# A two-layer transformer block on one core: last chunks by token halves, and a one-column stationary in the opening

## The reference, cut to what matters

```python
mod = silu(c) @ w_mod + b_mod                    # c is one row of 2048; w_mod 2048 x 12288
shift_a, scale_a, gate_a, shift_m, scale_m, gate_m = split(mod, 6)
h = rmsnorm(x, pre_mix_g) * (1 + scale_a) + shift_a
proj = h @ w_in
...                                              # latent attention, gated linear attention
x = x + gate_a * rmsnorm(mix @ w_out, post_mix_g)
h = rmsnorm(x, pre_mlp_g) * (1 + scale_m) + shift_m
x = x + gate_m * rmsnorm(relu(h @ w_up)**2 @ w_down, post_mlp_g)
# second block: rmsnorm, projections w_in_2, windowed attention and convolution, then
x = x + rmsnorm(merged @ w_out_2, mix_post_g_2)
x = x + rmsnorm((silu(gate) * up) @ w_down_2, ffn_post_g_2)   # gate, up = rmsnorm(x) @ w_gate_up_2
```

## Time and profile before

| | |
|---|---|
| median of three runs | 2870.9 us (2863.7 to 2878.3) |
| profiled execution | 2896.2 us, span 2894.4 us |
| TensorE busy, matmul and load | 95%, 81% |
| DVE, ScalarE, GpSimd busy | 64%, 42%, 1% |
| granted TensorE clock, mean | 0.965 of 2.4 GHz |
| HBM read | 560 MB, 194 GB/s over the span |

### The profile page before, as it was taken

How to read it: one execution, slowest core, us unless ns; L and a number is a source line. 1 busy time by engine, 2 the same in 40 slices (tenths; PEclk the granted TensorE clock), 3 DMA queues, 4 the chain that set the end, 5 groups by cost and what they waited for, 6 DMA issues and landing times.

```text
span 2894.4 us, 38739 instructions
## 1 busy us (share of the span) xinstructions
PE 2750.6 (95%) x14509; PEld 2357.5 (81%) x14509; DVE 1860.6 (64%) x2341; ACT 1214.6 (42%) x1553; POOL 21.9 (1%) x41
## 2 busy tenths in 40 slices
PE   7998899996999999999979999998979999999998
PEld 7886679885888888888768878887868888888886
DVE  4568788787986445654446878867455555655444
ACT  3144353144443444444344434454454444444443
POOL 1000000000000000000010000000000000000000
PEclk9789999997999999999989999999989999999999
DMA  7777786366786666665655645555545656655664
GB/s 260 269 273 260 231 251 208 102 214 237 241 282 196 196 191 187 186 189 192 195 138 169 193 140 169 169 155 170 175 129 183 187 183 188 186 183 182 192 194 152
DMA packets 434372, 564.19 MB, mean 195 GB/s; under 512 B 17959, under 2 KB 305123, under 8 KB 433744
## 3 DMA queue, kind: packets, MB, share of 16 engines
q1 hardware_dynamic: 432768, 559.76, 61.1%
q0 software_dynamic: 1488, 2.84, 0.4%
HBM read 560.43 MB, written 2.10 MB: 194 GB/s over the span
## 4 chain that ended last, share of the span: by engine, by line
PE 85%; DVE 6%; ACT 3%; DMA 3%; issue 2%; SPq 0%; ACTq 0%; DVEq 0%
PE ps L671 33%; PE ps L673 17%; PE ps L689 9%; PE ps L691 9%; PE ps L690 9%; PE ps L853 2%; DVE mod_acc L1521 2%; PE ps L994 2%; DMA mod_w<-in_w_mod 2%; DVE w_lo L1462 1%; ACT w_hi L1112 1%; DMA w_raw<-in_w_in 1%; ACT ring L1217 1%; DMA w_raw<-in_w_out 1%; PE ps L724 1%
## 5 line engine op out<-in xcount | busy, mean ns | idle before, releaser
L1462 DVE TENSOR_TENSOR w_lo<-w_raw,w_hi 128x1024 fp32r<-128x1024 f32 (+1 forms) x872 | 1052.6, 1212 | 763.5 <-ACT w_hi L1109 401.2
L671 PE MATMUL ps<-acts,w_hi 128*128 128x512 f32 x4224 | 1515.7, 403 | 16.3 <-DVE w_lo L1462 9.0
L673 PE MATMUL ps<-acts,w_lo 128*128 128x256 f32 x4224 | 1191.1, 282 | 0.0
L671 PEld LDWEIGHTS ps<-acts,w_hi 128*128 128x128 f32 x4224 | 801.7, 190 | 217.3 <-issue 17.4
L1112 ACT CAST w_hi<-w_raw 128x1024 fp32r<-128x1024 f32 (+2 forms) x560 | 580.8, 1042 | 725.5 <-PE ps L673 644.4
L673 PEld LDWEIGHTS ps<-acts,w_lo 128*128 128x128 f32 x4224 | 805.9, 191 | 2.2 <-issue 1.7
L1109 ACT CAST w_hi<-w_raw 128x1024 fp32r<-128x1024 f32 (+1 forms) x312 | 323.1, 1039 | 531.2 <-PE ps L691 399.1
L689 PE MATMUL ps<-w_hi,ff 128*128 128x512 f32 x864 | 336.3, 389 | 0.0
L691 PE MATMUL ps<-w_hi,ff 128*128 128x512 f32 x864 | 336.1, 389 | 0.0
L690 PE MATMUL ps<-w_lo,ff 128*128 128x512 f32 x864 | 336.1, 389 | 0.0
L690 PEld LDWEIGHTS ps<-w_lo,ff 128*128 128x128 f32 x864 | 162.2, 188 | 33.8
(11 more groups left out here) (278 smaller groups left out, 1773.7 us busy)
## 6 DMA issues: line engine op xcount, KB each, us to landing
w_raw<-in_w_in SPq DMA_DIRECT2D x232, 512.0 KB, 3.9
w_raw<-in_w_down SPq DMA_DIRECT2D x216, 512.0 KB, 4.3
mod_w<-in_w_mod SPq DMA_DIRECT2D x192, 512.0 KB, 5.4
w_raw<-in_w_gate_up SPq DMA_DIRECT2D x176, 512.0 KB, 3.6
w_raw<-in_w_up SPq DMA_DIRECT2D x128, 512.0 KB, 4.1
w_raw<-in_w_out SPq DMA_DIRECT2D x64, 512.0 KB, 4.6
w_raw<-in_w_attn_o SPq DMA_DIRECT2D x16, 512.0 KB, 3.6
w_raw<-in_w_conv_o SPq DMA_DIRECT2D x16, 512.0 KB, 4.1
```

The lines of the kernel that those rows point to most:

```text
L671: pe.matmul(ps[:, bank, :], hi, lin_.act[:, kk, :, :], start=at_first, stop=False, skip_group_check=True)
L673: mm = pe.matmul(ps[:, bank, 0:T], lo, lin_.act[:, kk, 0, :], start=False, stop=at_last, skip_group_check=True)
L1462: dve.tensor_tensor(low[cut], raw[cut], high[cut].bitcast(F32), ALU.subtract).then_inc(lo_ready, 1)
```

## The change

1. **Opening.** A scale piece is no longer eight matmuls with 128 columns of w_mod stationary and one column of silu(c) moving, but two with that column of silu(c) stationary and 512 columns of w_mod moving, summed into one row of PSUM bank 6. After a block's eight pieces ScalarE copies the row to `scale_row`, and `block_columns` (in place of `shift_sums`) turns it into four columns with one-row matmuls after the shift sums; both go to bank 7. Of the chunks of the block before, number 4 is now run ahead of the sums and not behind them.
2. **Token halves.** In the last panel of the four projections the last four chunks run for tokens 0 to 127 and then again for 128 to 255. Squares, roots, weighing, residual and scaling go by halves. The next phase's first four chunks are no longer rounded ahead but within the boundary: chunk 0 between the halves, chunks 1 to 3 between groups of four tiles. The transposes put two tiles in a bank and all of the first eight run without waiting for low parts. The stores go out by halves.

```diff
+        scale_row = mod_acc[0:1, 1, 0:NW]
...
+                self.first_half = count("first_half", 1)
+                self.half_added = count("y_half_added", 1 if partial else 0)
                 self.squared = count("y_squared", 8)
-                self.weighed = count("y_weighed", 4)
-                self.stat = count("y_stat", 3)
+                self.weighed = count("y_weighed", 5 if partial else 4)
+                self.stat = count("y_stat", 6)
...
+        last_of = {"w_or": o_1, "down_1": o_2, "out_2": o_3, "down_2": o_4}
...
+                half, quarter = divmod(g, 4)
...
-            def token_chunk(ph, j):
+            def token_chunk(ph, j, halves=(0, 1)):
...
-                pe.wait_ge(lo_ready, chunk_seq(ph, 0, j) + 1)
+                if halves[0] == 0:
+                    pe.wait_ge(lo_ready, chunk_seq(ph, 0, j) + 1)
...
-                    for half in range(2):
+                    for half in halves:
...
-                mm.then_inc(chunk_used, 1)
+                if halves[-1] == 1:
+                    mm.then_inc(chunk_used, 1)
+                elif j == ids[-1]:
+                    mm.then_inc(last_of[ph.name].first_half.sem, 1)
...
-                for j in chunk_ids(ph, b):
+                ids = chunk_ids(ph, b)
+                by_half = ids[-SLOTS:] if ph.name in last_of and b == ph.n_panels - 1 else []
+                for j in ids[:len(ids) - len(by_half)]:
                     if b == 0 and ph.name in ready:
                         pe.wait_ge(*ready[ph.name](sum(ph.chunks[j][1:])))
                     token_chunk(ph, j)
                     beside(ph, j, True)
+                for half in range(2):
+                    for j in by_half:
+                        token_chunk(ph, j, (half,))
...
-                    if k >= 4:
-                        pe.wait_ge(*(t.ring if t.shift else t.lo)(k - 3))
-                    pe.wait_ge(*t.scaled(2 * (k // 4) + 2))
+                    if k >= 8 and k % 2 == 0:
+                        pe.wait_ge(*(t.ring if t.shift else t.lo)(k - 6))
+                    pe.wait_ge(*t.scaled((3, 4, 6, 8)[k // 4]))
                     for half in range(2):
-                        mm = pe.transpose(ps[:, 4 + k % 4, half * P:(half + 1) * P],
-                                          t.xh[:, half, k * P:(k + 1) * P], ident)
+                        c = k % 2 * T + half * P
+                        mm = pe.transpose(ps[:, 4 + k // 2 % 4, c:c + P], t.xh[:, half, k * P:(k + 1) * P], ident)
                     mm.then_inc(t.turned.sem, 1)
...
-                if p == 0 and block >= 2:
-                    pe.wait_ge(mods_done, block - 1)
+                if p == 0 and block:
+                    pe.wait_ge(row_out, block)
                 for k in range(2):
-                    for i in range(4):
-                        mm = pe.matmul(ps[:, 6 + block % 2, i:i + 1],
-                                       mod_w[:, slot, k * NW + i * P:k * NW + (i + 1) * P],
-                                       silu_c[:, DT + 2 * p + k:DT + 2 * p + k + 1],
-                                       start=p == 0 and k == 0 and i == 0, stop=p == BLOCK_PIECES - 1 and k == 1,
-                                       skip_group_check=True)
+                    mm = pe.matmul(ps[0:1, 6, :], silu_c[:, DT + 2 * p + k:DT + 2 * p + k + 1],
+                                   mod_w[:, slot, k * NW:(k + 1) * NW], start=p == 0 and k == 0,
+                                   stop=p == BLOCK_PIECES - 1 and k == 1, skip_group_check=True)
                 mm.then_inc(scale_used, 1)
...
-            def shift_sums(block):
+            def block_columns(block):
                 pe.wait_ge(shift_used, 2 * BLOCK_PIECES * (block + 1))
+                if block:
+                    pe.wait_ge(mods_done, block)
                 for i in range(4):
-                    mm = pe.matmul(ps[:, 6 + block % 2, 4 + i:5 + i], mod_acc[:, 0, block % 2 * NW + i * P:block % 2 * NW + (i + 1) * P],
-                                   ones[:, 0:1], start=False, stop=True, skip_group_check=True)
+                    pe.matmul(ps[:, 7, 4 + i:5 + i],
+                              mod_acc[:, 0, block % 2 * NW + i * P:block % 2 * NW + (i + 1) * P],
+                              ones[:, 0:1], start=i == 0, stop=True, skip_group_check=True)
+                pe.wait_ge(row_out, block + 1)
+                for i in range(4):
+                    mm = pe.matmul(ps[:, 7, i:i + 1], scale_row[:, i * P:(i + 1) * P], ones[0:1, 0:1],
+                                   start=False, stop=True, skip_group_check=True)
                 mm.then_inc(mod_mm, 1)
...
-                shift_sums(0)
+                block_columns(0)
...
-                        opening_chunk(block - 2, 4)
                         opening_chunk(block - 2, 5)
...
-                    shift_sums(block)
-                opening_chunk(BLOCKS - 2, 4)
+                    opening_chunk(block - 1, 4)
+                    block_columns(block)
                 opening_chunk(BLOCKS - 2, 5)
...
+            def square_last(o, ph, half):
+                b = ph.n_panels - 1
+                act.wait_ge(*o.squared(2 * b + half))
+                if o.partial:
+                    if half:
+                        act.wait_ge(summed, panel_seq(ph, 0, b) + 1)
+                    else:
+                        act.wait_ge(*o.half_added(1))
+                    src = o.y[:, half, b * NW:(b + 1) * NW]
+                else:
+                    if half:
+                        act.wait_ge(chunk_used, chunk_seq(ph, 0, ph.n_chunks - 1) + 1)
+                    else:
+                        act.wait_ge(*o.first_half(1))
+                    src = ps[:, 2 * bank_pair(ph, b) + half, :]
+                act.activation(square, src, ACT.Square,
+                               accum_out=y_sums[:, half, b:b + 1]).then_inc(o.squared.sem, 1)
+            def square_stream(o, t, half):
+                for quarter in range(4):
+                    n = 4 * half + quarter
+                    act.wait_ge(*o.added(n + 1))
+                    if quarter:
+                        act.wait_ge(*t.squared(n))
+                    act.activation(square, x_tok[:, half, quarter * NW:(quarter + 1) * NW], ACT.Square,
+                                   accum_out=x_sums[:, half, quarter:quarter + 1]).then_inc(t.squared.sem, 1)
+            def scale_half(t, half, quarter):
+                act.wait_ge(*t.stat(3 * half + 3))
+                cut = slice(quarter * NW, (quarter + 1) * NW)
+                act.activation(t.xh[:, half, cut], x_tok[:, half, cut], ACT.Identity,
+                               scale=x_root[:, half:half + 1]).then_inc(t.scaled.sem, 1)
...
+                    act.wait_ge(scale_used, BLOCK_PIECES * block)
+                    if block > 1:
+                        act.wait_ge(mod_mm, block - 1)
+                    act.copy(scale_row, ps[0:1, 6, :]).then_inc(row_out, 1)
...
+            def boundary(o, t, before, ph):
+                square_last(o, before, 0)
+                root(y_root[:, 0:1], o.stat, 0)
+                square_stream(o, t, 0)
+                act.wait_ge(*t.squared(4))
+                square_last(o, before, 1)
+                root(x_root[:, 0:1], t.stat, 0)
+                root(y_root[:, 1:2], o.stat, 1)
+                scale_half(t, 0, 0)
+                round_chunk(ph, 0, 0, True)
+                square_stream(o, t, 1)
+                root(x_root[:, 1:2], t.stat, 1)
+                scale_half(t, 1, 0)
+                scale_half(t, 0, 1)
+                scale_half(t, 1, 1)
+                for quarter in range(4):
+                    if quarter:
+                        round_chunk(ph, 0, quarter, True)
+                    turn_high(t, range(4 * quarter, 4 * quarter + 4))
+                    if quarter < 2:
+                        scale_half(t, 0, quarter + 2)
+                        scale_half(t, 1, quarter + 2)
+            def finish(o, ph):
+                for half in range(2):
+                    square_last(o, ph, half)
+                    root(y_root[:, half:half + 1], o.stat, half)
...
+            def half_root(sums, ap, stat, half):
+                link(dve.tensor_reduce(ap[:, half:half + 1], sums[:, half, :], AX.X, ALU.add))
+                dve.tensor_scalar(ap[:, half:half + 1], ap[:, half:half + 1], 1.0 / D, EPS, ALU.mult,
+                                  ALU.add).then_inc(stat.sem, 1)
+            def half_inverse(ap, stat, half):
+                dve.wait_ge(*stat(3 * half + 2))
+                dve.reciprocal(ap[:, half:half + 1], ap[:, half:half + 1]).then_inc(stat.sem, 1)
+                dve.wait_ge(*stat(3 * half + 3))
+            def add_last(o, ph, half):
+                b = ph.n_panels - 1
+                if o.partial:
+                    if half:
+                        dve.wait_ge(chunk_used, chunk_seq(ph, 0, ph.n_chunks - 1) + 1)
+                    else:
```

(70 more changed lines are left out.)

120 lines of the change are left out of this document (44 added, 76 removed).

## The result

| | before | after |
|---|---|---|
| median, runs of the two side by side | 2877.5 us (2863.7 to 2880.1, 5 runs) | 2856.8 us (2848.8 to 2857.7, 5 runs) |
| ratio, with 95% interval | | 0.9932 (0.9907 to 0.9957): 12 to 27 us faster |
| the same, measured again with the experiments | 2879.1 us (30 runs) | 2854.8 us (7 runs), 0.9934 (0.9909 to 0.9958) |
| profiled execution, span | 2894.4 us | 2847.0 us |

The change gains about 20 us (19 to 20 by the two ratios, 21 and 24 by the two pairs of medians). 38 were forecast, 2833 us. The two profiled executions differ by 47.4 us: the first profile of before (2896.2 us) was 18.8 us above the mean of all the 70 runs of that kernel that there are by now (2877.4 us), and above each of them.

What follows compares the result with a forecast made beforehand. TensorE was taken as the bound, 85% of the span, with its clock lowered in the opening. 27 us there and 10.7 at the boundaries made 38 off a median of 2870.9: 2833 us, range 2818 to 2860.

Steps and rivals of the forecast that it cites:

- block 0: First block of the opening: 11.9 us gained at full clock, nothing at half clock; 8 us taken.
- the block by hand: Opening, engine timeline worked out: block 1 takes 31.3 us, blocks 2 and 3 take 33.9 us each.
- The clock: Opening: the new scale pieces keep TensorE at 2.4 GHz in blocks 1 to 3, 1.72 us a piece.
- the thin stationary: Opening: the reason given for the clock holding, a stationary of few columns and all 128 rows.
- Rival (a): Opening: load round trips through two slots set the blocks, 2.8 us gained in each of three; 2852 us, chance 0.18.
- The tail: After the opening's last block: 0.5 us gained, as chunk 0 waits for its mods with only chunk 5 as cover.
- The boundaries: Ends of the four projections: half 0's norm runs under pass two; 1.0 + 3.4 + 3.4 + 2.9 = 10.7 us gained.
- the 1.7 to be given back at the bias loads: Second boundary: TensorE's wait grows from 2.3 to 4.0 us, cutting the gain of 5.1 to 3.4.
- (b): Opening: one stationary column does not hold the clock, every piece takes 3.4 us; 18 us slower, 2889 us, chance 0.07.
- (c): Boundaries: the smaller stock of loaded chunks gives gains back, 4 us left in all; 2840 us, chance 0.13.
- the signs to look for: After-profile: clock near 1.00, 34 us blocks, no load lull over 2 us, transposes at 9 to 10 us, 8 us end.
- The chances for faster: Whole kernel: 0.85 for faster, from the forecast (0.62), (c) and two thirds of Rival (a).

Runs made afterwards that it cites:

- halves alone: The kernel before with only the token halves edits, its opening left as it was: 2863.8 us, ratio 0.9944 to the kernel before.
- opening alone: The kernel before with only the opening's edits, its boundaries left as they were: 2865.3 us, ratio 0.9966 to the kernel before.
- new order: The changed kernel with chunk roundings and remainders reordered at the three inner boundaries, chunk 0 under the second pass: 2844.6 us, 0.9881 of before.
- eight slots: The changed kernel with eight slots for the opening's pieces in place of four: 2833.2 us, ratio 0.984 to the kernel before.
- the run with a wide one: The changed kernel with silu(c)'s column repeated 128 times as stationary, still 512 columns moving: 2854.9 us, 0.991 of before.

## Why the prediction was wrong, point by point

The opening by stretches, in us. "Old" is the mean of four profiles with the old opening (before three times, halves alone), "new" of four with the new one (opening alone, after twice, new order). Their ranges for block 0 are 44.6 to 51.6 and 38.4 to 40.2.

| | old | new | gained | forecast |
|---|---|---|---|---|
| block 0 | 48.1 | 39.4 | 8.6 | 8 |
| block 1 | 35.5 | 35.2 | 0.4 | 4.3 |
| block 2 | 39.3 | 36.7 | 2.6 | 7.3 |
| block 3 | 39.8 | 35.5 | 4.3 | 7.1 |
| behind it | 38.0 | 40.5 | -2.5 | 0.5 |
| sum | 200.7 | 187.3 | 13.4 | 27 |

**The step that failed** is the block by hand, 31.3 and 33.9 us: it laid out the loads through two slots too early, and TensorE's own work at its shortest. The three blocks come out at 35.2, 36.7 and 35.5 us, 8.3 us more in all. The working let the pieces' loads land 5.3 to 5.6 us behind the issue. The load behind piece 2, which stands on the chain in each of blocks 1 to 3, takes 6.54, 6.86 and 6.61 us in the first profile of after. In block 2 it is issued at 88.95 behind loads that are still under way, the last of which lands at 94.50, and it lands at 95.81; the loads ahead of it come in 1.3 to 1.4 us apart as well. The two loads on the chain make 1.2 of the 1.9 us by which block 2 is too long, and the rest is TensorE's own: on the chain its pieces take 1.82 to 1.88 us for 1.72, and a chunk takes 2.9 for 2.7.

The working had 3.8 us of waiting for loads (0.8, 1.9 and 1.1) in a block of 33.9, and in blocks 2 and 3 TensorE's idle time is not above that (3.5 and 2.8 by the mean of the four). What grew there is its busy time, 33.2 and 32.8 us for 30.1: longer pieces and chunks, and after half of the waits of 2 us and more a slip to 1.2 GHz, which the working did not have. In block 1 three of the four profiles begin with 1.8 to 2.4 us of waiting for DVE's last shift part, and in the first profile of after the load of that part (4.72 us) stands on the chain ahead of it. With eight slots the blocks are 0.5, 2.2 and 2.2 us below the working, so it is the two slots that cost it.

The clock, the step that the prediction doubted most, was right in size: blocks 1 to 3 together were granted 0.94 to 0.98. Its reason, the thin stationary, was not (the run with a wide one). Rival (a), with a chance of 0.18, named the round trip, and its price for the three blocks, 8.4 us, stands beside 7.3 measured. That the two agree is in part luck: it had 2.8 for each block, and 0.4, 2.6 and 4.3 were gained. It was dismissed because the lulls in the earlier trace rows show SyncE waiting for TensorE. They do, and in the changed kernel too. Both hold in turn: early in a block the loads run dry while TensorE works up to piece 0, and later they queue at 400 GB/s while TensorE waits. Rival (a) in turn was wrong to give block 0 nothing.

Block 0 gained 8.6 for 8, and that is luck in part: the prediction had it end at 43.6 in place of 51.6. It ends at 39.4, near the 39.7 worked out for full clock, in place of 48.1.

**The second part of the error is the sample.** Blocks 2 and 3 were taken at 41.2 and 41.0 us from one profile; the mean of four is 39.3 and 39.8, 3.1 us less to gain. That profile was 25 us above the median shown, and the prediction took its microseconds off the median without asking where the 25 lay. 13 of the 21 us by which it exceeds the two later ones lay in the opening. The median of three was itself 6.5 us below the mean of 70 runs, so 2833 would have been 2839 from that base.

**The tail** of the opening, 0.5 gained by the forecast, lost 2.5. TensorE waits 2.10 us up to 154.93 for the first remainder of the last block: with chunk 4 ahead of the sums only chunk 5 covers the way over DVE and ScalarE. The wait was named and priced at nearly nothing. The row of after, and then the tail with all engines in after, with chunk 4 behind the sums, and with eight slots:

```profile
154.93 0.47 PE L696 MATMUL ps<-w_hi,acts 128*128 128x512 f32 x1 [2.10 <-DVE w_lo L1535]
...
146.16:186.68 40.52, 36.72 (x174) 30.74 (x174) 22.61 (x36) 23.52 (x35) 0.00 (x0) 0.96 0.62 223
...
149.92:190.56 40.64, 38.06 (x173) 32.55 (x173) 23.12 (x37) 23.62 (x35) 0.00 (x0) 0.92 0.65 221
...
131.57:170.51 38.94, 35.13 (x173) 29.56 (x173) 22.28 (x35) 23.52 (x35) 0.00 (x0) 1.00 0.58 204
```

The wait alone does not make the loss. With chunk 4 behind the sums it is gone, and the tail is still 40.6 us, at a granted clock of 0.92. In this profile with eight slots the wait is there but the clock is not lowered, and the tail is 38.9. So the wait and the clock behind it cost the 2.5 us together, and putting chunk 4 back does not win them.

Together 8.3 + 3.1 + 3.0 - 0.6 (block 0 gave a little more) = 13.8, which is the 13.6 us missing in the opening up to rounding.

**The boundaries** were right in mechanism and close in size, 10.7 forecast. By chunk 2 behind the last matmul: first 37.5 to 33.9, less 2.4 to 3.6 us by which w_or ends later (44.4 to 44.7 us from the spreading of the row to the last matmul with the old kernel, 47.1 to 48.0 with the changed one; but also 47.2 with the opening alone and 47.5 with the halves alone, so it is not shown whose it is), so 0 to 1 for 1.0. Second 31.7 to 26.1, 5.6 for 5.1, and the 1.7 to be given back at the bias loads was not given back, the wait staying at 2.0 and 2.3 in the two profiles. Third 29.2 to 26.2, 3.0 for 3.4. End 10.85 to 7.3, 3.5 for 2.9. In all 12 to 13, and 16 (9 to 23) by the runs of the halves alone. Measured up to the first bias product the second boundary gives more: 210.2 to 214.7 us in the four profiles with the old boundaries, 203.7 to 206.1 in the eight with the halves in their first order, 7.5 by the means.

**Rivals.** (b) fell: 1.86 us a piece, 2.66 would have been needed. (c) fell for the change as it stands and shows only in the shorter boundary of the new order. Of the signs to look for, the clock, the 9 us to the transposes, the 3 us of waiting for DVE and the 8 us at the end came; the blocks of 34 us and the wait of 4 us at the bias loads did not. The load line came out between: the lull of block 2 is down to under 2 us, but in block 3 nothing is moved from 117.0 to 119.25.

**Its sums.** The lower end of the range, 2818, needs the upper bound of 35 us for the opening and 17 for the boundaries; block 0 wholly at full clock gives 31 and 2823. The chances for faster add up to 0.87 and not 0.85. Neither touches the forecast.

What is left between 26 (opening and boundaries by the means of profiles, 13.4 + 12 to 13) and 19 to 24 by the runs is inside the intervals; it was not traced further.

## What to carry to other kernels

A bound that is lifted uncovers the next one: before crediting a stage with what its engine is spared, lay out the loads as the new, faster engine would ask for them, with everything in flight at the same time, and see which piece waits for which slot. Price a change against several executions; where the profiled one is far above the median, find the stretch that holds the excess first, since it may be the one that is to be changed. And when the gain stays small, try the next bound with one edit: four more slots turned some 10 us into 24.

## What the runs showed of the hardware

**Two rates at one clock.** In the loop of gate_up TensorE is busy without a break, granted 1.00 throughout, and does the same work; yet it has two rates, and an execution keeps one of them to the end of the loop. All engines between 2160 and 2600 us: busy and count of TensorE matmuls, loads, DVE, ScalarE, GpSimd, then clock, DMA share, GB/s. First after, then before (a second profile):

```profile
2160.00:2600.00 440.00, 440.00 (x2536) 388.23 (x2535) 265.45 (x277) 197.56 (x221) 0.00 (x0) 1.00 0.63 189
```

```profile
2160.00:2600.00 440.00, 440.00 (x2492) 381.56 (x2491) 260.84 (x273) 192.56 (x215) 0.00 (x0) 1.00 0.59 186
```

2536 matmuls against 2492 in the same 440 us, 1.8%. From the first chunk behind the third boundary to the last matmul it makes 9.3 us. Of the 14 profiles six have the higher rate, six of the nine with the new opening and none of the five with the old one, too few to say whether the two are linked. The edits do not touch this loop. The rate is 9.3 us of the 47.4 between the first two profiles. What sets it was not found, and if it hung on the new opening, part of the gain in the medians would be its.

**The opening's clock differs from run to run.** With the same code block 0 took 51.6, 45.6 and 44.6 us in three executions, with 27.91 us of busy matmuls in its pieces in the first and 24.76 and 24.89 in the others: the first stayed at 1.2 GHz throughout, the others rose to 2.4 before the block was over.

**Read rate.** The kernel with eight slots read 386 GB/s over a whole block of 30.8 us, with single slices at 408. The Trainium skill ("DMA: Bandwidth & Descriptors", Specifications) gives about 358 GB/s as a core's share; the single core goes past it here. Its section Measured says as much: with the pair's other core idle its figures, for loads issued from GpSimd, reach 425.
